# The projections of a recurrent layer in another order, its neighbour mean by halves, and the first block's preparation placed between the products of v

## What is computed

```python
def centred_shift(x):
    xp = jnp.pad(x, ((0, 0), (1, 1), (0, 0)))
    return 0.5 * (xp[:, :-2] + xp[:, 2:])

def rwkv_prepare(h, mu, w_rkv, w0, w1, w2, a0, a1, a2, g1, g2, k_k, k_a):
    xx = centred_shift(h) - h
    xr, xw, xk, xv, xa, xg = h[None] + xx[None] * mu[:, None, None, :]
    r, k, v = jnp.einsum('sbtd,sde->sbte', jnp.stack([xr, xk, xv]), w_rkv)
    w_logit = w0[...] + einsum('zbtr,zrd->zbtd', jnp.tanh(einsum('btd,zdr->zbtr', xw, w1)), w2)
    decay = jnp.exp(-jnp.exp(-jax.nn.softplus(-w_logit) - 0.5))
    a = jax.nn.sigmoid(a0[...] + einsum('zbtr,zrd->zbtd', einsum('btd,zdr->zbtr', xa, a1), a2))
    g = jax.nn.sigmoid(xg @ g1) @ g2
    kk = split_heads(k * k_k, RW_HEADS, RW_HEAD_DIM)
    kk = (kk / jnp.maximum(jnp.linalg.norm(kk, axis=-1, keepdims=True), 1e-12)).reshape(k.shape)
    k_dir = k[None] * (1.0 + (a - 1.0) * k_a)
    return r, k_dir, v, decay, -kk, kk[None] * a, g

def step(s, inp):                      # rwkv7_scan, one token
    rt, wt, kt, vt, at, bt = inp
    sa = jnp.einsum('bhij,bhj->bhi', s, at)
    s = s * wt[:, :, None, :] + sa[..., None] * bt[:, :, None, :] + vt[..., None] * kt[:, :, None, :]
    return s, jnp.einsum('bhij,bhj->bhi', s, rt)
```

## Time and profile before

| | |
|---|---|
| time, median of 3 runs | 3303.9 us (3303.23 to 3305.49) |
| time of the profiled execution | 3304.01 us |
| its span, first to last instruction | 3302.2 us |
| mean granted clock of PE | 0.95 of full speed |

### The profile page before, as it was taken

How to read it: one execution, slowest core, us unless ns; L and a number is a source line. 1 busy time by engine, 2 the same in 40 slices (tenths; PEclk the granted TensorE clock), 3 DMA queues, 4 the chain that set the end, 5 groups by cost and what they waited for, 6 DMA issues and landing times. The chain is left out here.

```text
span 3302.2 us, 55139 instructions
## 1 busy us (share of the span) xinstructions
PE 3038.7 (92%) x24496; PEld 2349.9 (71%) x24496; DVE 1695.1 (51%) x2652; ACT 1040.9 (32%) x1658; POOL 293.9 (9%) x391
## 2 busy tenths in 40 slices
PE   7999997999988959899979999999899999998999
PEld 3864333798975438888958989774689897455797
DVE  2334365656553038777646555454454554564453
ACT  2233201333331044434213333322333333142332
POOL 2320010000000022322210000000000000200000
PEclk9999898999999979999979999999999999998999
DMA  8323443355543010000124545542255555413353
GB/s 256 94 102 128 153 153 110 124 197 181 179 144 128 26 26 3 3 3 3 37 76 172 179 155 187 194 153 102 78 174 175 173 179 168 146 59 128 102 179 128
DMA packets 249926, 409.26 MB, mean 124 GB/s; under 512 B 10151, under 2 KB 102712, under 8 KB 249560
## 3 DMA queue, kind: packets, MB, share of 16 engines
q1 hardware_dynamic: 244824, 390.39, 34.9%
q0 software_dynamic: 4864, 15.35, 1.8%
HBM read 400.67 MB, written 2.95 MB: 122 GB/s over the span
## 5 line engine op out<-in xcount | busy, mean ns | idle before, releaser
L346 DVE TENSOR_TENSOR ring_parts<-ring,arena_parts 128x2048 fp32r<-128x2048 f32 x250 | 553.1, 2254 | 277.3 <-ACT arena_parts L339 275.2
L339 ACT CAST arena_parts<-ring 128x2048 fp32r<-128x2048 f32 x250 | 457.8, 1883 | 587.3 <-PE psum L2491 229.8
L2491 PE MATMUL psum<-arena_parts 128*128 128x256 f32 x2816 | 512.5, 285 | 1.9 <-DVE arena_parts L571 1.5
L2491 PEld LDWEIGHTS psum<-arena_parts 128*128 128x128 f32 x2816 | 443.6, 194 | 3.4 <-DVE arena_parts L571 2.7
L2491 PE MATMUL psum<-arena_parts,ring_parts 128*128 128x256 f32 x1408 | 400.5, 284 | 0.0
L383 PE MATMUL psum<-arena_parts 128*128 128x512 f32 x928 | 288.8, 393 | 10.8 <-DVE arena_parts L2527 8.2
L2491 PEld LDWEIGHTS psum<-arena_parts,ring_parts 128*128 128x128 f32 x1408 | 272.8, 194 | 0.0
L1614 PE MATMUL psum<-arena_parts 128*128 128x512 f32 x768 | 239.3, 393 | 7.8 <-DVE arena_parts L1663 7.8
L684 PE MATMUL psum<-ring,hT 128*128 128x512 f32 (+1 forms) x512 | 221.2, 593 | 5.6 <-DVE hT L1535 2.6
L383 PEld LDWEIGHTS psum<-arena_parts 128*128 128x128 f32 x928 | 175.2, 189 | 48.5 <-DVE arena_parts L2527 9.0
L1596 PE MATMUL psum<-arena_parts 128*128 128x256 f32 x1024 | 192.2, 290 | 4.0 <-DVE arena_parts L579 2.1
(11 more groups left out here) (446 smaller groups left out, 5464.4 us busy)
## 6 DMA issues: line engine op xcount, KB each, us to landing
ring<-in_mlp_w SPq DMA_DIRECT2D x48, 2048.0 KB, 8.2
ring<-in_ada_w SPq DMA_DIRECT2D x24, 2048.0 KB, 8.0
ring<-in_ffn_pre_w_gu SPq DMA_DIRECT2D x44, 1024.0 KB, 7.2
ring<-in_ffn_post_w_gu SPq DMA_DIRECT2D x44, 1024.0 KB, 7.3
ring<-in_ffn_pre_w_down SPq DMA_DIRECT2D x8, 2048.0 KB, 8.2
ring<-in_xmem_wkv SPq DMA_DIRECT2D x8, 2048.0 KB, 8.0
ring<-in_ffn_post_w_down SPq DMA_DIRECT2D x8, 2048.0 KB, 7.8
ring<-in_ab_w_in SPq DMA_DIRECT2D x7, 2048.0 KB, 7.8
```

What stands on the lines that cost most here:

```text
L339: nc.scalar.copy(high_view(name)[:, k, :], raw_view(name)[:, k, :]).then_inc(*up(act, ("high", name, h)))
L346: nc.vector.tensor_tensor(low_view(name)[:, k, :], raw_view(name)[:, k, :], high_view(name).bitcast(F32)[:, k, :], ALU.subtract)\
L2491: ins = nc.tensor.matmul(psum[:, b, 256 * j:256 * j + 256], s[:, k, at:at + P], x_parts[q][:, k, :], start=(k == 0 and i == 0), stop=(k == ...
```

## The change

- The order of the projections becomes g, r, w, a, k, v, and the slabs are planned in that order (g1, rw_r, w1, a1, rw_k, rw_v).
- `mix_dve` forms the neighbour mean in two halves, `shift(0)` for the latent tokens behind the latent norm, `shift(1)` for the context tokens behind the context norm. Between them stand the mixing of g, the second row tile of the context norm, the mixing of r and the context norm's output. On PE the context norm's turn moves behind g1, on ACT its output moves behind the sigmoids of g.
- The context norm now uses banks 4 to 7 like the others.
- v's rows go to two areas, one for each half of the channels, through banks 5, 6 and 7 in turn. POOL's 16 transfers become 32 of half the size.
- Block 0 is prepared during the products of v: on PE between them (`prep_pe(pe, 0, ...)` in `proj_pe`), on ACT in `first_prep_act`, which puts each copy of v's rows at a chosen tick (`VALUES_AFTER`), on DVE right behind the mixing. Its waits are for k ("mix used", 4) instead of VS, and for the first v slab (FIRST_OUT - 2) ahead of the first write to Kh. Slot -1 shrinks to its last seven ticks. The waits for VS move to DVE's A of block 1 and to PE's first walk.

```diff
+        plan_rows("g1", a["rw_g1"][0], KT, 160)
+        plan_rows("rw_r", a["rw_w_rkv"][0, 0], KT, D)
         for w in ("w1", "a1"):
...
-        v_rows = area(0, 4, 1024)
+        v_rows = (area(20480, 4, 512), area(2560, 4, 512))
...
-        MIXES = ("w", "a", "g", "r", "k", "v")
+        MIXES = ("g", "r", "w", "a", "k", "v")
...
+            for n in range(2):
+                for t in range(4):
+                    pool.wait_ge(*when(("rw", "mix used", 5)))
+                    pool.wait_ge(*when(("rw_v", "rows", n, t)))
+                    for hh in range(2):
+                        for par in range(2):
+                            nc.gpsimd.dma_start(VS[HH[hh], 2 * t + par, 4 * n:4 * n + 4, :],
+                                                v_rows[n][HH[par], t, :].rearrange("p (f h d) -> p f h d", f=4, h=2)[:, :, hh, :])\
+                                .then_inc(landing("VS"), 16)
...
+            def shift(half):
+                stage(dve, "mix")
                 for k in range(KT):
-                    dve.wait_ge(*when(((key, "part"), k)))
...
+                    dve.wait_ge(*when(((("L1a", "C1a")[half], "part"), k)))
+                hh, ss = h[:, half::2, :], shifted[:, half::2, :]
+                nc.vector.tensor_tensor(ss[:, :, 1:255], hh[:, :, 0:254], hh[:, :, 2:256], ALU.add).then_inc(*up(dve))
+                nc.vector.tensor_copy(ss[:, :, 0:1], hh[:, :, 1:2]).then_inc(*up(dve))
+                nc.vector.tensor_copy(ss[:, :, 255:256], hh[:, :, 254:255]).then_inc(*up(dve))
+                dve.wait_ge(*latest(dve))
+                nc.vector.scalar_tensor_tensor(ss, ss, 0.5, hh, ALU.mult, ALU.subtract).then_inc(*up(dve))
+                dve.wait_ge(*latest(dve))
...
+            shift(0)
+            mix(0)
+            norm_tile_dve(dve, "C1a", 1)
+            mix(1)
+            norm_out_dve(dve, "C1a")
+            shift(1)
+            for i in range(2, 6):
+                mix(i)
...
                     if m == "g":
+                        norm_turn_pe(pe, "C1a")
+                        stage(pe, "proj")
...
-                    rows_pe(pe, "rw_v", lambda k, t: mixed[1][:, k, P * t:P * t + P], range(4), KT, D, [0, 1, 2, 3])
-                    stage(pe, "proj")
+                    prep_pe(pe, 0, -7)
+                    prep_pe(pe, 0, -5)
+                    for n in range(2):
+                        for t in range(4):
...
+                            pe.wait_ge(*bank(v_bank(n, t), ("rw_v", n, t)))
+                            for k in range(KT):
+                                ins = nc.tensor.matmul(psum[:, v_bank(n, t), :], x_[:, k, P * t:P * t + P], s[:, k, :],
+                                                       start=(k == 0), stop=(k == 7))
+                            ins.then_inc(*up(pe, ("rw_v", "full", n, t)))
+                            if (n, t) == (0, 0):
+                                prep_pe(pe, 0, -3)
+                            if (n, t) == (1, 0):
+                                prep_pe(pe, 0, 12)
...
+        def v_bank(n, t):
+            return 5 + (4 * n + t) % 3
...
+        def first_prep_act(act):
+            for tick in range(-7, 8):
+                prep_act(act, 0, tick)
+                if tick in VALUES_AFTER:
+                    values_act(act, *divmod(VALUES_AFTER.index(tick), 4))
+            for i in range(len(VALUES_AFTER), 8):
+                values_act(act, *divmod(i, 4))
+
+        VALUES_AFTER = (-4, -1, 2, 4, 7)
...
-                act.wait_ge(*when(("dma", "VS")))
-                act.wait_ge(*when(("used", FIRST_OUT - 1)))
+                act.wait_ge(*when(("rw", "mix used", 4)))
...
-                    dve.wait_ge(*when(("dma", "VS")))
-                    dve.wait_ge(*when(("rw", "mix used", 5)))
-                    dve.wait_ge(*when(("used", FIRST_OUT - 1)))
+                    dve.wait_ge(*when(("rw", "mix used", 4)))
...
+                if f == 0 and z == 0:
+                    dve.wait_ge(*when(("used", FIRST_OUT - 2)))
                 dve.wait_ge(*when(("sigmoids", f, z)))
...
+                if f == 1 and z:
+                    dve.wait_ge(*when(("dma", "VS")))
...
+            if f == 0 and hop == 0:
+                pe.wait_ge(*when(("dma", "VS")))
...
             norm_turn_pe(pe, "L1a")
-            norm_turn_pe(pe, "C1a")
             proj_pe(pe)
             for tick in range(EARLY, TICKS):
-                prep_pe(pe, 0, tick - TICKS)
-            for f in range(-1, 9):
+                near_pe(pe, 0, tick)
+                prep_pe(pe, 1, tick - TICKS)
+            for f in range(9):
                 slot_pe(pe, f)
...
             rw_pool(pool)
-            for f in range(-1, 9):
+            for tick in range(EARLY, TICKS):
+                near_pool(pool, 0, tick)
+            for f in range(9):
                 slot_pool(pool, f)
```

72 lines of the change are left out of this document (32 added, 40 removed).

## The result

The changed kernel takes 3283.0 us in the median of four runs (3276.73 to 3286.53), the one before 3304.69 in the same comparison (3303.23 to 3308.33). The ratio is 0.9932, with a 95% interval of 0.9916 to 0.9948: 21.7 us faster, where 34 had been forecast, and 2 us outside the range (3262 to 3281). The profiled execution of the changed kernel is the fastest of its runs, 3276.73 (span 3274.9). Both traces are read here, since what they differ by is part of the answer.

What follows compares the result with a forecast made beforehand. PE, busy 92%, was taken to lose time in idle gaps and at low clock. With POOL's queue then binding, its second inversion step came 33.2 us earlier: 3304.0 - 33.2 = 3270.8, with part of a scan 3270; range 3262 to 3281.

Steps and rivals of the forecast that it cites:

- part of a scan: DVE's late scan of block 1 would fit into PE's wait for POOL, adding up to 1.2 us of gain.
- g at 990.7: Start of projections: g needs only the latent half, so its first product could start at 990.7, not 999.93.
- The mixings of w, a and k under their covers: Projections: DVE's mixings hide under PE's g2, r and a; a's has 1.7 us of margin.
- The pause ahead of v: Between k and v: block 0's first rates and ACT's exponential delay v from 1110.2 to 1114.2.
- kk and coef as no waits: Block 0's products among v's: PE waits for neither; coef is ready at 1148.5, wanted at 1149.8.
- The way from the end of v to the step without the queue: End of v to PE's second inversion step if POOL's transfers did not hold it: 10.9 us, to 1181.8.
- The rival that issues beside busy engines cost 1.10: POOL's 32 VS issues take 35.2 us beside busy engines, the gain falls to 17.2, time 3286.8; chance 0.10.
- I let the two cancel: PE's second inversion step: the clock falls in the wait for POOL, but today's 1.76 is already below full speed; net nothing.
- I charge g the same 1.76: g's first product after PE's idle gap: low clock adds 1.76 us to 7.26.
- the shift goes through to the end: Behind PE's second inversion step: slots 0 to 8 do the same work, so the 33.2 us gain reaches the end.
- its signs of being wrong: Profile after: no POOL wait, a stall before k or after v's fifth product, issues above 0.7 us, or slots 1 to 8 changed.
- the fourth: A projection margin breaks, early clock costs more, or the halved mean gains nothing: 3273 to 3279; chance 0.12.

Runs made afterwards that it cites:

- e0: Changed kernel run again with no edit: 3285.24 us, ratio 0.9938 to the kernel before.
- e1: Changed kernel with the 32 VS transfers issued by SP instead of POOL: 3276.24 us, ratio 0.9912 to the kernel before.
- e10: Changed kernel with identity products filling both PE's gap ahead of g (40) and its wait for POOL (42): 3266.51 us, ratio 0.9888 to the kernel before.
- e6: Changed kernel with 40 unused identity products in PE's gap ahead of g: 3271.99 us, ratio 0.9907 to the kernel before.
- e2: Changed kernel with kind 1's rates and kk each one product of v later: 3280.03 us, ratio 0.9923 to the kernel before.
- e3: Kernel before with only the new projection order, halved neighbour mean and moved context turn; block 0 prepared the old way: 3303.86 us, ratio 0.9995.
- e5: Changed kernel with VS transfers on SP and kind 1's rates and kk one product of v later: 3266.59 us, ratio 0.9886 to the kernel before.
- e7: Changed kernel with each of the 32 VS transfers cut in two, 64 issues: 3292.95 us, ratio 0.9985 to the kernel before.
- e9: Changed kernel with the old projection order, undivided mean and context turn in its old place: 3282.4 us, ratio 0.9937 to the kernel before.
- e14: Kernel before with six more repeats of DVE's first transpose of block 0's near matrix, as a delay: 3310.2 us, ratio 1.0009.
- e4: Kernel before run again with no edit, for a second profile: 3304.3 us in one run.

## Why the prediction was wrong

The sum was 3304.0 - 33.2, rounded to 3270 with part of a scan. Against e0, which is near the median: the step at 1197.48 instead of 1191.8, 5.7 us (0.8 of them older than the changed stretch); from there to the last sum 385.2 instead of 380.7, 4.5; rest 1699.8 instead of 1696.5, 3.3; the part of the scan, 0.8. Together 14.3, and 3284.29 - 3270 is 14.3. Against the first profiled execution: 3.4, 2.5 and 0, with the 0.8 the 6.7 that 3276.73 stands above 3270. That this one execution falls into the range is luck: it is the fastest of ten.

**Right, to within a microsecond:** g at 990.7 (990.90). Turn, g2, r, w, a and k without a wait, with k 54.8 long (55.1, from 1056.15 to 1111.25). The mixings of w, a and k under their covers. The pause ahead of v (4.0 said, 4.3 measured). kk and coef as no waits. The size of an issue (0.60 said, 0.61), POOL's start (0.37 us behind v) and the sum behind it. PE standing some 10 us for POOL (11.84 in all). The way from the end of v to the step without the queue (10.9 said, 10.8 in e1, where PE waits 1.36 instead of 11.8). The rival that issues beside busy engines cost 1.10 fell: 32 took 19.53 us, 0.61 each, although DVE worked for 6.92 us of that time and ACT for 11.98. The mechanism that the Trainium skill's page "SBUF — State Buffer" warns of in its note on the "DVE blocks DMA" trap left no mark in that row; whether DVE was ever in the mode that the note speaks of, no row shows.

**Right in size, by the clock:** "The clock will fall in that wait; but [...] I let the two cancel." They do, within 1 us. The inversion's four steps from the second on, up to PE's next work, took 5.3 us before (1225.02 to 1230.32), 5.0 in the first trace of the changed kernel (1195.25 to 1200.28) and 6.0 in e0 (1197.48 to 1203.44), and from the step to the third sum it was 37.4, 37.1 and 38.0. e10 shows another thing, that both kernels lose there: with the wait filled, the four steps took 3.8 (1190.92 to 1194.70).

**Wrong, two steps, both of the clock:**

1. "The clock has fallen by then too, so I charge g the same 1.76." The charge was mis-sized. g1 takes 10.11 and 10.21 us against 7.29 in e6 at 1.00: 2.8 to 2.9. And the prediction put two further low stretches at nothing. One lies in g2 and r (3.2 us in e0, e2 and e3, 4.9 in e1, e5 and e7), the other in v's first product, behind the 2.11 us pause (after: 8.83 against 7.13, 1.7). So the step came late by 3.4 in the first trace (1.1 of g1, 1.7 of v) and by 5.7 in e0 (0.8 at the start, 1.1 of g1, 3.2 of g2 and r); 0.6 or 0.7 is left in each.
2. "Behind this point nothing in any engine's order changes, so the shift goes through to the end." The order indeed doesn't change, and the time does. The recurrence took 375.9 to 385.6 us in the seventeen profiles, the rest 1696.5 or 1699.8, with the same instructions. Between the third sum and the ninth, before took 168.2 us at a clock of 0.95, the changed kernel 171.0 at 0.93 and 172.2 at 0.92 (e0); the second profile of before took 165.1 at 0.97. This is the larger part of the miss against e0: 4.5 and 3.3 of the 14.3 us. It can go the other way too: a step later by 19.1 us became 8.4 at the end (e7 against e0), and one later by 4.3 became 1.1 less (e9 against e0). The prediction had named this among its signs of being wrong: slots 1 to 8 of another length than now.

Of the rivals, the fourth (3273 to 3279, 0.12) was true in its mechanism: "the early clock costs more". Its price stood on top of the queue's, as it should, but it held only the loss ahead of the step. The range's upper end, 3281, allowed for the projections' gain to go and not for the slower passage behind it.

**Open.** What decides which execution gets how many low stretches in the recurrence and near 2410 and 2540; whether the changed kernel's recurrence (383.2 and 385.2) is slower than before's (377.5 and 380.7) by something in the change: with block 0 prepared the old way it took 377.5 to 381.1 us in seven profiles, the new way 375.9 to 385.6 in ten, which overlap; and why the low stretch in g2 and r goes when the gap ahead of it is filled.

## What to carry to other kernels

A shift worked out at one place is not yet a shift at the end. In a kernel that is bound by PE and has waits of a few microseconds in it, what lies behind may run at another clock, and a gain of a few microseconds can vanish or double; take two profiles of the kernel before, and let what they differ by stage for stage (here 3.2 and 3.3 us) widen the range. Charge an idle gap of PE not only with its length but with the low clock behind it, and look for gaps that remain after a change: filling the one ahead of g was worth some 8 to 13 us here, while the reordered projections without it were worth nothing that could be measured. In the kernel before, a fill that ended 2.2 us ahead of the work gained nothing, so a fill has to be measured and not assumed. Many small transfers on one queue are paid by the issue, so put them on the queue whose next instruction nobody waits for.

## What the runs showed of the hardware

- The granted clock fell to 1.2 GHz while PE was busy: in e0 PE works 14.00 of 14 us at 0.98 and then 7.00 of 7 at 0.51. In e3 it is 13.00 of 13 us at 1.00 and then 8.00 of 8 at 0.57, at the same place. In the first profile of the changed kernel, with the same instructions, that stretch is at 1.00, and one in v's first product is low. In e14, whose code there is the kernel before's, PE works 8.00 of 8 us from 1034 at 0.57, where before is at 1.00.
- Over slots 1 to 3 the same 4038 matmul records took 165.1 us at a mean clock of 0.97 and 172.2 at 0.92 (e4 and e0).
- Two executions of one program, 0.3 us apart in their spans, differ by 3.2 us in the recurrence and 3.3 in the rest, in opposite directions.
- An issue on GpSimd's queue costs 0.68, 0.61 and 0.58 us at 8, 4 and 2 pieces a row and 64 rows.
- Identity products (128 by 128, f32) leave two matmul records each of 0.11 us: 40 of them fill 9.10 us of the gap, and the clock at the end of the gap is 1.00.
